# RWKV-7's triangular inverse on one Trainium2 core: the inverse, its transpose and the gram's product carried through the doubling levels

## The reference, cut to what matters

```python
def step(S, inp):
    r_t, w_t, k_t, v_t, kk_t, a_t = inp
    sa = jnp.einsum('bhvk,bhk->bhv', S, -kk_t)
    S = S * w_t[:, :, None, :] + sa[..., None] * (kk_t * a_t)[:, :, None, :] + v_t[..., None] * k_t[:, :, None, :]
    return S, jnp.einsum('bhvk,bhk->bhv', S, r_t)
```

## Time and profile before

| | |
|---|---|
| time, median of 3 runs (lowest, highest) | 2323.49 us (2321.61, 2324.8) |
| the profiled execution: time, span | 2326.79 us, 2325.0 us |
| PE busy | 2274.8 us (98%) |
| PE weight loads | 1737.7 us (75%) |
| DVE busy | 1068.3 us (46%) |
| ACT busy | 661.3 us (28%) |
| POOL busy | 1743.7 us (75%) |
| granted TensorE clock, mean | 0.997 of full |

### The profile page before, as it was taken

How to read it: one execution, slowest core, us unless ns; L and a number is a source line. 1 busy time by engine, 2 the same in 40 slices (tenths; PEclk the granted TensorE clock), 3 DMA queues, 4 the chain that set the end, 5 groups by cost and what they waited for, 6 DMA issues and landing times. The chain is left out here.

```text
span 2325.0 us, 38356 instructions
## 1 busy us (share of the span) xinstructions
PE 2274.8 (98%) x16032; PEld 1737.7 (75%) x16032; DVE 1068.3 (46%) x1411; ACT 661.3 (28%) x1193; POOL 1743.7 (75%) x1228
## 2 busy tenths in 40 slices
PE   7999999999999999999999999999999999999999
PEld 5767777777777778777777677777777777777777
DVE  5023337556454762555250232455464547534542
ACT  5222222222221322343341223222132213314421
POOL 3677679678578989888537666876686789898784
PEclk9999999999999999999999999999999999999999
DMA  4622344333234545632445232533332344466323
GB/s 159 191 83 78 112 136 118 92 93 116 73 105 146 150 144 181 235 95 77 145 108 170 82 105 77 162 94 96 93 115 88 87 156 144 145 199 221 88 81 127
DMA packets 165487, 288.64 MB, mean 124 GB/s; under 512 B 28792, under 2 KB 36344, under 8 KB 163776
## 3 DMA queue, kind: packets, MB, share of 16 engines
q1 hardware_dynamic: 125216, 211.60, 30.9%
q10 hardware_dynamic: 40096, 74.57, 9.6%
HBM read 234.43 MB, written 51.68 MB: 123 GB/s over the span
## 5 line engine op out<-in xcount | busy, mean ns | idle before, releaser
L747 POOL TENSOR_SCALAR w_hi<-raw 128x512 fp32r<-128x512 f32 x552 | 908.2, 1645 | 379.6 <-PE ps_proj L788 322.8
L757 POOL TENSOR_TENSOR w_lo<-raw,w_hi 128x512 fp32r<-128x512 f32 (+1 forms) x640 | 841.0, 1315 | 154.5 <-ACT w_hi L1242 99.1
L788 PE MATMUL ps_proj<-h_hi,w_hi 128*128 128x512 f32 (+1 forms) x1760 | 726.7, 413 | 9.9 <-ACT stage L1235 6.3
L788 PE MATMUL ps_proj<-h_lo,w_hi 128*128 128x512 f32 (+1 forms) x1760 | 689.9, 392 | 0.0
L788 PE MATMUL ps_proj<-h_hi,w_lo 128*128 128x512 f32 x1728 | 676.5, 391 | 0.0
L788 PEld LDWEIGHTS ps_proj<-h_hi,w_hi 128*128 128x128 f32 (+1 forms) x1760 | 330.1, 188 | 106.6 <-issue 27.3
L788 PEld LDWEIGHTS ps_proj<-h_lo,w_hi 128*128 128x128 f32 (+1 forms) x1760 | 329.9, 187 | 73.8 <-DVE h_lo L1758 0.4
L788 PEld LDWEIGHTS ps_proj<-h_hi,w_lo 128*128 128x128 f32 x1728 | 326.2, 189 | 66.5 <-issue 7.7
L803 PE MATMUL ps_proj<-w_hi,h_hi 128*128 128x512 f32 x448 | 181.0, 404 | 0.4 <-POOL w_lo L757 0.4
L803 PE MATMUL ps_proj<-w_hi,h_lo 128*128 128x512 f32 x448 | 174.8, 390 | 0.0
L803 PE MATMUL ps_proj<-w_lo,h_hi 128*128 128x512 f32 x448 | 174.6, 390 | 0.0
(11 more groups left out here) (349 smaller groups left out, 2962.1 us busy)
## 6 DMA issues: line engine op xcount, KB each, us to landing
raw<-in_w_in_dram SPq DMA_DIRECT2D x480, 256.0 KB, 2.7
raw<-in_w_out_dram SPq DMA_DIRECT2D x128, 256.0 KB, 2.9
projected<-stage SPq DMA_DIRECT2D x116, 256.0 KB, 2.7
arena<-projected ACTq DMA_DIRECT2D x90, 256.0 KB, 3.2
out_dram<-arena ACTq DMA_DIRECT2D x7, 1024.0 KB, 4.8
gated_hi<-arena ACTq DMA_DIRECT2D x24, 256.0 KB, 2.8
gated_lo<-arena ACTq DMA_DIRECT2D x24, 256.0 KB, 3.2
h_hi<-gated_hi SPq DMA_DIRECT2D x8, 768.0 KB, 5.5
```

Source lines behind the costliest of these rows:

```text
L747: nc.gpsimd.tensor_scalar(hi, src, 1.0, None, ALU.mult).then_inc(s_hi_split, 1)
L757: nc.gpsimd.tensor_tensor(lo, src, hi.bitcast(F32), ALU.subtract).then_inc(s_raw_split, 1)
L788: last = mm(ps_proj[rows, m, :], lhsT, rhs, start=(k == 0 and j == 0), stop=(k == KT - 1 and j == len(products) - 1))
```

## The change

Three matrices are carried through the levels in place of one and its transpose: R = the product of the gram with X (`rw_r`), its transpose Rt, and Xt (both in `rw_rx`, side by side, 128 columns a matrix). X itself is no longer stepped. With y the masked R, a level makes one block "step_r" (Rt^T y, the update of R) and one block of y with [Rt | Xt] (128 columns; the last two levels 64). DVE then subtracts the update of R from `rw_r` in three pieces, masks it (now from SBUF), and subtracts the updates of Rt and of Xt in three pieces each. Pieces: head 0 on all partitions (128x256), head 1 on either half of the partitions (64x256), crossing from the other half of PSUM (`ACROSS`). ACT no longer takes part in the levels, apart from three copies of R at the start. DVE has 44 operations a head pair in this part where it had 10, ACT 3 where it had 5 (L1500 and four of L1507).

PE's blocks a head pair: before 1 of 8 products (L1018), 13 of 16, and the last (L1059) of 16 with only half of the array's quarters in turn; after 8 of 16 products of 64 columns and 3 of 16 products of 128 columns. Places for projection tiles a head pair: before `rw_level` 5x1, `rw_step` 4x1, `rw_levels` 1, after `rw_first_level` 2, `rw_level` 3x4, `rw_last_level` 3, `rw_levels` 2: 19 tiles where there were 10. The 36 tiles a layer come out of `to_z_da` (28, which ends a group and is now empty) and `da_first` (20, now 12); `ml_qk` of head 2 gives 3 to `ml_rest` of head 1. The diff, cut (indentation shortened; `planned()` places the new names in the order of PE's program, and the transposes at L1003 and L1006 and DVE's L1900 and L1901 use `rw_xt_level`):

```diff
+STEPS_OF_X = 6 * len(LEVELS) - 3
+ACROSS = ((slice(0, 64), slice(64, 128)), (slice(64, 128), slice(0, 64)))
...
-rw_gram=(4, 4, 4, 4), rw_x=(2, 2, 2, 2), rw_level=(1, 1, 1, 1), rw_step=(1, 1, 1, 1), rw_levels=(1, 1, 1, 1),
+rw_gram=(4, 4, 4, 4), rw_x=(2, 2, 2, 2), rw_first_level=(2, 2, 2, 2), rw_level=(4, 4, 4, 4), rw_last_level=(3, 3, 3, 3), rw_levels=(2, 2, 2, 2),
-ml_first=25, ml_qk=(19, 6, 13, 13), ml_s=(8, 8, 8, 8), ml_h=(3, 3, 3, 3), ml_gate=(0, 0, 9, 0), ml_rest=(22, 15, 6, 12),
-da_first=20, da_sums=(14, 10, 10, 10), da_scores=(6, 6, 6, 6), da_half=(15, 17, 17, 17), da_turned=(3, 3, 3, 3),
+ml_first=25, ml_qk=(19, 6, 10, 13), ml_s=(8, 8, 8, 8), ml_h=(3, 3, 3, 3), ml_gate=(0, 0, 9, 0), ml_rest=(22, 18, 6, 12),
+da_first=12, da_sums=(14, 10, 10, 10), da_scores=(6, 6, 6, 6), da_half=(15, 17, 17, 17), da_turned=(3, 3, 3, 3),
...
 rw_xt, rw_x, rw_y, rw_pu = r2(8, 64), r2(8, 64), r2(8, 64), r2(8, P)
+rw_r, rw_rx = r2(8, 64), r2(8, P)
+rw_rt, rw_xt_level = rw_rx[:, :, 0:64], rw_rx[:, :, 64:P]
...
         for q, o in swapped:
             mm(ps[q, 2, own], rw_gk[q, i, 0:64], rw_vT[q, i, 0:64], start=True, stop=True)
-            mm(ps[o, 3, 256 + i * 64:256 + (i + 1) * 64], rw_gk[q, 4 + i, 0:64], rw_vT[q, i, 64:P],
+            last = mm(ps[o, 3, 256 + i * 64:256 + (i + 1) * 64], rw_gk[q, 4 + i, 0:64], rw_vT[q, i, 64:P],
                start=True, stop=True)
-
-    for i in range(NT):
-        for q, o in swapped:
-            last = mm(ps[o, 3, i * 64:(i + 1) * 64], ident[q, q], rw_xt[q, 4 + i, :],
-                      start=True, stop=True)
     last.then_inc(s_rw_x_first, 1)
     fill("rw_x", hp)
-    pe.wait_ge(s_rw_x_ready, 5 * hp + 5)

     n_levels = len(LEVELS)
-    for lv in range(n_levels):
-        if lv:
-            pe.wait_ge(s_rw_x_stepped, (n_levels - 1) * hp + lv)
+
+    def step_r(rt, by):
         for i in range(NT):
             own = slice(i * 64, (i + 1) * 64)
             for q, o in swapped:
-                mm(ps[q, 0, own], rw_gb[q, i, 0:64], rw_x[q, i, :], start=True, stop=True)
-                last = mm(ps[o, 1, own], rw_gb[q, 4 + i, 0:64], rw_x[q, 4 + i, :],
-                          start=True, stop=True)
+                mm(ps[q, 0, own], rt[q, i, 0:64], by[q, i, :], start=True, stop=True)
+                last = mm(ps[o, 1, own], rt[q, 4 + i, 0:64], by[q, 4 + i, :], start=True, stop=True)
         last.then_inc(s_rw_levelled, 1)
-        if lv:
-
-            for i in range(NT):
-                own = slice(i * 64, (i + 1) * 64)
-                for q, o in swapped:
-                    mm(ps[q, 2, own], rw_x[q, i, :], ident[q, q], start=True, stop=True)
-                    last = mm(ps[o, 3, own], rw_x[q, 4 + i, :], ident[q, q], start=True, stop=True)
-            last.then_inc(s_rw_xt_mm, 1)
-        fill("rw_level", hp, lv)
+
+    pe.wait_ge(s_rw_x_ready, 4 * hp + 2)
+    step_r(rw_gb, rw_x)
+    pe.wait_ge(s_rw_x_ready, 4 * hp + 4)
+    for i in range(NT):
+        own = slice(i * P, i * P + 64)
+        for q, o in swapped:
+            mm(ps[q, 2, own], rw_x[q, i, :], rw_gb[q, i, 0:64], start=True, stop=True)
+            last = mm(ps[o, 3, own], rw_x[q, 4 + i, :], rw_gb[q, 4 + i, 0:64], start=True, stop=True)
+    last.then_inc(s_rw_xt_mm, 1)
+    fill("rw_first_level", hp)
+    for lv in range(n_levels):
         pe.wait_ge(s_rw_level_masked, n_levels * hp + lv + 1)
-        if lv:
-            pe.wait_ge(s_rw_xt_stepped, n_levels * hp + lv)
+        pe.wait_ge(s_rw_xt_stepped, STEPS_OF_X * hp + (6 * lv if lv else 3))
         if lv < n_levels - 1:
-            for i in range(NT):
-                fed = slice(256 + i * 64, 256 + (i + 1) * 64)
-                for q, o in swapped:
-                    mm(ps[q, 0, fed], rw_xt[q, i, :], rw_y[q, i, :], start=True, stop=True)
-                    last = mm(ps[o, 1, fed], rw_xt[q, 4 + i, :], rw_y[q, 4 + i, :],
-                              start=True, stop=True)
-            last.then_inc(s_rw_x_mm, 1)
-            fill("rw_step", hp, lv)
-    for i in range(NT):
-        own = slice(i * 64, (i + 1) * 64)
-        for q, o in swapped:
-            mm(ps[q, 2, own], rw_y[q, i, :], rw_xt[q, i, :], start=True, stop=True)
-            last = mm(ps[q, 3, own], rw_y[q, 4 + i, :], rw_xt[q, 4 + i, :], start=True, stop=True)
-    last.then_inc(s_rw_xt_mm, 1)
+            step_r(rw_rt, rw_y)
+        if 0 < lv < n_levels - 1:
+            pe.wait_ge(s_rw_xt_stepped, STEPS_OF_X * hp + 6 * lv + 3)
+        of = 0 if lv < n_levels - 2 else 64
+        for i in range(NT):
+            own = slice(i * P + of, (i + 1) * P)
+            for q, o in swapped:
+                mm(ps[q, 2, own], rw_y[q, i, :], rw_rx[q, i, of:P], start=True, stop=True)
+                last = mm(ps[o, 3, own], rw_y[q, 4 + i, :], rw_rx[q, 4 + i, of:P], start=True, stop=True)
+        last.then_inc(s_rw_xt_mm, 1)
+        if lv < n_levels - 2:
+            fill("rw_level", hp, lv)
+        elif lv < n_levels - 1:
+            fill("rw_last_level", hp)
     fill("rw_levels", hp)
-    pe.wait_ge(s_rw_xt_stepped, n_levels * (hp + 1))
+    pe.wait_ge(s_rw_xt_stepped, STEPS_OF_X * (hp + 1))
     for i in range(NT):
...
-    nc.scalar.activation(rw_xt[:, 4:8, :], ps[:, 3, 0:256].rearrange("p (i c) -> p i c", i=NT), ACT.Copy).then_inc(s_rw_x_ready, 1)
     fill("rw_x", hp)
-    n_levels = len(LEVELS)
-    for lv in range(n_levels):
-        if lv:
-            act.wait_ge(s_rw_xt_mm, n_levels * hp + lv)
-            xt = rw_xt.rearrange("p (h i) c -> p h (i c)", h=2)
-            nc.scalar.activation(xt, ps[:, 2:4, 0:256], ACT.Copy).then_inc(s_rw_xt_stepped, 1)
+    act.wait_ge(s_rw_levelled, len(LEVELS) * hp + 1)
+    pieces = "p (i c) -> p i c"
+    nc.scalar.activation(rw_r[:, 0:4, :], ps[:, 0, 0:256].rearrange(pieces, i=NT), ACT.Copy).then_inc(s_rw_r_copied, 1)
+    for to, of in ACROSS:
+        nc.scalar.activation(rw_r[to, 4:8, :], ps[of, 1, 0:256].rearrange(pieces, i=NT), ACT.Copy).then_inc(s_rw_r_copied, 1)
+    fill("rw_first_level", hp)
+    for lv in range(len(LEVELS) - 2):
         fill("rw_level", hp, lv)
-        if lv < n_levels - 1:
-            fill("rw_step", hp, lv)
+    fill("rw_last_level", hp)
     fill("rw_levels", hp)
...
     n_levels = len(LEVELS)
-    for lv in range(n_levels):
-        level_mask = levels[:, lv * 64:(lv + 1) * 64]
-        dve.wait_ge(s_rw_levelled, n_levels * hp + lv + 1)
-        by_head = "p (h i) c -> p h i c"
-        v.tensor_tensor(rw_y.rearrange(by_head, h=2), ps[:, 0:2, 0:256].rearrange("p h (i c) -> p h i c", i=NT), level_mask[:, None, None, :].to_broadcast([P, 2, NT, 64]), MUL).then_inc(s_rw_level_masked, 1)
-        if lv < n_levels - 1:
-            dve.wait_ge(s_rw_x_mm, (n_levels - 1) * hp + lv + 1)
-            x = rw_x.rearrange("p (h i) c -> p h (i c)", h=2)
-            v.tensor_tensor(x, x, ps[:, 0:2, 256:512], SUB).then_inc(s_rw_x_stepped, 1)
-    dve.wait_ge(s_rw_xt_mm, n_levels * (hp + 1))
-    xt = rw_xt.rearrange("p (h i) c -> p h (i c)", h=2)
-    v.tensor_tensor(xt, xt, ps[:, 2:4, 0:256], SUB).then_inc(s_rw_xt_stepped, 1)
+    pieces = "p (i c) -> p i c"
+    r_products = [ps[:, h, 0:256].rearrange(pieces, i=NT) for h in range(2)]
+    x_products = [ps[:, 2 + h, :].rearrange(pieces, i=NT) for h in range(2)]
+
+    def mask_of(lv, n):
+        return levels[:, None, lv * 64:(lv + 1) * 64].to_broadcast([P, n, 64])
+
+    def step(dst, part):
+        v.tensor_tensor(dst[:, 0:4, :], dst[:, 0:4, :], x_products[0][:, :, part], SUB).then_inc(s_rw_xt_stepped, 1)
+        for to, of in ACROSS:
+            v.tensor_tensor(dst[to, 4:8, :], dst[to, 4:8, :], x_products[1][of, :, part], SUB).then_inc(s_rw_xt_stepped, 1)
+
+    r_part, x_part = slice(0, 64), slice(64, P)
+    dve.wait_ge(s_rw_xt_mm, (n_levels + 1) * hp + 1)
+    v.tensor_copy(rw_rt[:, 0:4, :], x_products[0][:, :, r_part]).then_inc(s_rw_xt_stepped, 1)
+    for to, of in ACROSS:
+        v.tensor_copy(rw_rt[to, 4:8, :], x_products[1][of, :, r_part]).then_inc(s_rw_xt_stepped, 1)
+    dve.wait_ge(s_rw_r_copied, 3 * (hp + 1))
+    v.tensor_tensor(rw_y, rw_r, mask_of(0, 8), MUL).then_inc(s_rw_level_masked, 1)
+    for lv in range(n_levels - 1):
+        dve.wait_ge(s_rw_levelled, n_levels * hp + lv + 2)
+        link(v.tensor_tensor(rw_r[:, 0:4, :], rw_r[:, 0:4, :], r_products[0], SUB))
+        for to, of in ACROSS:
+            link(v.tensor_tensor(rw_r[to, 4:8, :], rw_r[to, 4:8, :], r_products[1][of], SUB))
+        dve.wait_ge(s_rw_xt_mm, (n_levels + 1) * hp + lv + 2)
+        v.tensor_tensor(rw_y, rw_r, mask_of(lv + 1, 8), MUL).then_inc(s_rw_level_masked, 1)
+        if lv < n_levels - 2:
+            step(rw_rt, r_part)
+        step(rw_xt_level, x_part)
+    dve.wait_ge(s_rw_xt_mm, (n_levels + 1) * (hp + 1))
+    v.tensor_tensor(rw_xt[:, 0:4, :], rw_xt_level[:, 0:4, :], x_products[0][:, :, x_part], SUB).then_inc(s_rw_xt_stepped, 1)
+    for of, to in ACROSS:
```

(1 more changed line is left out.)

17 lines of the change are left out of this document (8 added, 9 removed).

## The result

The changed kernel takes 2356.98 us (median of 4 runs, 2355.55 to 2358.17) against 2324.14 for the kernel before beside it: ratio 1.0142, 95% interval 1.0125 to 1.0160. It is slower by 32.8 us where I had forecast 18.8. The direction and most terms held; the time lies 4 us above the range. The profiled execution has a span of 2356.4, 31.3 more than before.

What follows compares the result with a forecast made beforehand. PE's instruction stream plus its waits was taken to bound the kernel. Levels -20.8 + 20.0, group ends +6.8 and attention's start +12.8 sum to +18.8, from 2323.5 to 2342.3 us; range 2322 to 2353.

Steps and rivals of the forecast that it cites:

- The levels: Head pairs' levels: PE saves 2.6 a head pair (20.8 us), waits for DVE give back 2.5 (20.0).
- Xt is late: In the levels PE waits for Xt from DVE: 0.55 in level 1, 0.26 each in levels 2 and 3.
- Pieces without a wait in series: DVE's subtractions in the levels run one after another, 0.42 apart, not overlapping.
- The mask: DVE's mask in a level, both inputs now in SBUF, takes 0.87, bounds 0.69 and 1.1.
- Group ends: Tiles 560 and 688 end groups where ACT is busy: PE waits 2.3 and 1.1 a layer, 6.8 us together.
- Attention's start, to L1176: Differential attention's start with 24 tiles of cover, not 60: PE waits 4.9 a layer for the squares.
- From L1176 to the scores: Differential attention, first block to scores: data ready at 907.8, PE done at 906.3, so 1.5 more a layer.
- The three tiles within mLSTM: Moving three tiles in mLSTM keeps 28 tiles between the same two heads and costs nothing.
- the lost cover costs nothing: Rival at attention's start and two group ends: moved tiles cost no time there, kernel faster, 2309.5 us; chance 0.12.
- the pieces overlap: Rival in the levels: DVE pieces overlap, mask short, waits 6.8 to 11, about 2331 us; chance 0.20.
- Rival 3: In the levels, DVE pieces dearer than 0.42 or mask at 1.1: waits 28, 2350 us and above; chance 0.09.

Runs made afterwards that it cites:

- e2: The kernel before with the changed kernel's layout of projection tiles, no operation changed: 2358.0 us, ratio 1.0132 to 1.0162.
- f5: The changed kernel with the second pair of heads subtracted in one VectorE instruction on 128 partitions instead of two crossing ones (wrong halves): 2338.0 us, ratio 1.0055 to 1.0085.
- h1: The changed kernel with swapped rows loaded before the squares and unread products in TensorE's wait for the squares: 2348.9 us, ratio 1.0092 to 1.0143.
- f1: The changed kernel with the loads of the swapped rows issued before the squares of q and k, not after: 2354.0 us, ratio 1.0124 to 1.0154.
- e4: The changed kernel with products that nobody reads placed in TensorE's first two waits of differential attention: 2357.2 us, ratio 1.0127 to 1.0168.
- e1: The changed kernel, all operations kept, with the projection tiles laid out as before the change: 2380.5 us, ratio 1.0228 to 1.0259.

## Why the prediction was right where it was, and where it failed

- **The levels.** Right in size and in kind: TensorE's saving of 2.6 a head pair and VectorE's waits cancel (-0.8 forecast, -0.6 measured). The two terms hold one by one, though the list of waits has only 14.8 of the 20.0. Under the same tiles the old levels (e2) take 26.5 a head pair, without a wait, and f5, which has the new products and in three of its eight head pairs no wait, 23.9 there: 2.6 saved. The changed kernel's eight take 213 against 8 x 23.9: 22 us of waits. Its blocks of levels 1 and 2, a block of level 1 in f5, and e2's stretch:

```profile
611.25:613.29 2.04, 1.73 (x65) 1.43 (x64) 1.88 (x6) 0.00 (x0) 1.96 (x2) 1.00 0.02 6
616.24:617.98 1.74, 1.74 (x66) 1.43 (x65) 1.52 (x5) 0.00 (x0) 1.66 (x2) 1.00 0.05 9
```

```profile
604.74:606.24 1.50, 1.50 (x65) 1.33 (x64) 0.78 (x3) 0.00 (x0) 1.42 (x2) 1.00 0.18 67
```

```profile
599.79:626.26 26.47, 26.47 (x559) 19.92 (x559) 6.90 (x10) 5.73 (x12) 16.57 (x13) 1.00 0.34 102
```

So Xt is late by 0.54 in level 1 (0.55 forecast) and 0.24 in level 2 (0.26). PE's record has only 0.31 of these 0.78 as idle time and the rest as busy time inside the block, so the list of waits doesn't show it. Pieces without a wait in series at 0.45: right, f5 priced them. The mask was 0.80 on the mean (0.87 taken), the level 4.67 (4.7). The rule from VectorE: DVE Perf Modes of the Trainium skill (section "Two Vector instructions with no wait between them"), on which pieces go in series, agrees with these rows.
- **Group ends.** Right: TensorE waits 2.2 us at tile 560 and 1.0 at 688, in both layers (2.3 and 1.1 forecast). ACT, and PE's next tile behind it, layer 0:

```profile
547.13 1.97 ACT L1232 ACTIVATE stage<-ps_proj 128x512 f32<-128x512 f32 x3 [0.28 <-PE ps_proj L791]
549.12 1.28 ACT L1275 ACT_TABLE_LOAD   x1
...
553.61 0.58 ACT L1232 ACTIVATE stage<-ps_proj 128x512 f32<-128x512 f32 x1
...
554.24 0.50 PE L791 MATMUL ps_proj<-w_hi,h_hi 128*128 128x512 f32 x1 [2.17 <-ACT stage L1232]
```

- **Attention's start, to L1176.** Right: 4.2 and 5.3 measured where I had 4.9 a layer.
- **From L1176 to the scores: the step that failed.** I had 1.5 a layer by carrying the old chain over (12.8 from L1614 to the scores' data, 14 tiles in 9.7); it was 3.8 and 4.0. With it the start of differential attention cost 17.4 us where I had 12.8 and a bound of 15. Two sizes were off. The rows of after (answers the earlier trace rows):

```profile
921.00 0.72 ACT L1610 ACTIVATE arena<-arena,par 128x512 f32<-128x512 f32 x1
...
923.17 1.49 ACTq L1603 DMA_DIRECT2D stage<-projected  x4
...
930.28 0.87 DVE L2043 SCALAR_TENSOR_TENSOR arena<-stage,par,arena 128x512 f32<-128x512 f32 x1 [18.39 <-DMA stage<-projected]
...
935.76 1.69 DVE L2049 TENSOR_TENSOR arena<-arena 128x512 f32<-128x512 f32 x1
```

The swapped rows are in use 7.1 after their issue in place of 5.5, while the DMA engines are full (share 1.00, 377 GB/s in the 6.8 us above), and L2049 takes 1.69 in place of 1.00: it ended 0.55 behind a subtraction of GpSimd that had started 0.15 before it, as the masks of the last section do. That loads are slower because SP catches up behind the wait is argued from these rows; no run varied it. Beside it lay the halved clock, which h1's trace shows to be a second, parallel cost of some 3 us a layer (14.45 in f1, 11.49 in h1, layer 0).
- **No term for the clock.** Behind the scores of layer 1 (a wait of 2.3, then 6.8 us at half) it cost 3.0. That and the 4.6 above are 7.6 of the 12.5 us that the forecast lacks in the span; 3.7 more stand in mLSTM of layer 1.
- **The three tiles within mLSTM "cost nothing".** Not refuted. The 3.7 of layer 1 are two waits of L1143 (1.7 and 2.4, where the kernel before has 0.5 and 1.3) and 1.5 of halved clock. But e2 and e4, with the same three tiles moved, wait 0.4 and 1.1, and 0.5 and 1.1 there. The waits differ between executions, and nothing ties them to the tiles; why they differ stays open.
- The rival "the lost cover costs nothing" is refuted by e2, that the pieces overlap by the rows and f5. Rival 3's time came true for another reason than its own. That one is luck. My range took its upper end from the bounds of levels and start: the levels stayed inside theirs, the start went past its own by 2.4, and the cost of the clock, which no term named, had no bound at all.

## What to carry to other kernels

A tile of cover has a price where it is taken, and it can be as large as the whole change: price a change's operations and its rescheduling in two separate kernels (e1 and e2) before judging either, and expect the two prices not to add up. Where two things end a wait at nearly the same time, an experiment on one of them shows nothing; undo both before calling one innocent. In a chain across the partitions' sides, count VectorE's instructions, not its elements. And a list of waits can leave out pauses inside a block of matmuls (it has 14.8 us of 22 here): compare the length of the stretch with that of a kernel that doesn't wait there.
